# Seven products of constants on TensorE between one expert pair's down product and the next pair's gate/up

## The reference, cut to what matters

```
def per_seq(args):
    xi, gi = args
    hid = jax.nn.silu(jnp.einsum('sd,edf->sef', xi, w_gate)) * jnp.einsum('sd,edf->sef', xi, w_up)
    return jnp.einsum('sef,se,efd->sd', hid, gi, w_down)
```

## Time and profile before

| | |
|---|---|
| median of 3 runs | 774.24 us (773.31 to 775.62) |
| profiled execution, its own time | 774.24 us |
| its span, first to last instruction | 772.6 us |
| TensorE busy | 709.6 us, 92% |
| mean granted clock | 0.964 |
| moved by DMA | 150.31 MB |

### The profile page before, as it was taken

The page is one execution under the profiler, slowest core; times in us unless marked ns, Lnnn a source line. Parts: engine busy times, 40 slices in busy tenths (PEclk is TensorE's granted clock), DMA queues, the critical chain, the costliest instruction groups (busy, mean ns, idle before and its releaser), DMA issues.

```text
span 772.6 us, 10496 instructions
## 1 busy us (share of the span) xinstructions
PE 709.6 (92%) x3892; PEld 476.4 (62%) x3892; DVE 380.6 (49%) x758; ACT 279.3 (36%) x648; POOL 145.4 (19%) x126
## 2 busy tenths in 40 slices
PE   6999999999999999999999999988999786868784
PEld 5867888788888888666566688876433232323221
DVE  6876777785868723766776553471212110111100
ACT  4934633544454445544554432221212110211100
POOL 3513331330301102000120032011122111111111
PEclk9999999999999999999999999977999898989988
DMA  8333212330303122500110059798999999999972
GB/s 279 84 110 109 92 36 93 108 95 14 108 3 109 53 88 78 212 8 1 52 59 2 1 197 419 316 375 316 407 402 404 393 407 416 404 413 408 387 281 42
DMA packets 44038, 150.31 MB, mean 195 GB/s; under 512 B 11557, under 2 KB 11649, under 8 KB 32209
## 3 DMA queue, kind: packets, MB, share of 16 engines
q1 hardware_dynamic: 38384, 134.61, 45.5%
q0 software_dynamic: 4720, 8.70, 4.6%
q10 hardware_dynamic: 880, 6.30, 2.0%
HBM read 145.09 MB, written 12.88 MB: 204 GB/s over the span
## 4 chain that ended last, share of the span: by engine, by line
PE 67%; SPq 15%; DVE 6%; DMA 6%; ACT 3%; issue 2%; POOL 0%; POOLq 0%; ACTq 0%; DVEq 0%
PE bank L1093 13%; PE bank L1095 12%; PE bank L1094 12%; SPq L367 10%; PE bank L1483 6%; SPq L383 4%; DMA s_gu<-in_w_expert_up_dram 4%; PE bank L1507 3%; PE bank L1330 3%; PE bank L1302 2%; PE bank L1316 2%; PE bank L1472 2%; DVE s_wl L261 2%; PE bank L1210 2%; PE bank L1306 1%
## 5 line engine op out<-in xcount | busy, mean ns | idle before, releaser
L1483 PE MATMUL bank<-s_gu,s_xgT 128*64 128x512 f32 x448 | 110.3, 649 | 29.7 <-DMA s_gu<-in_w_expert_up_dram 29.7
L261 DVE TENSOR_TENSOR s_wl<-s_raw,s_wh 128x512 fp32r<-128x512 f32 x84 | 88.5, 1092 | 25.9 <-ACT s_wh L772 25.6
L1483 PEld LDWEIGHTS bank<-s_gu,s_xgT 128*64 128x64 f32 x448 | 36.6, 149 | 102.2 <-issue 102.2
L772 ACT ACTIVATE s_wh<-s_raw 128x512 fp32r<-128x512 f32 x120 | 74.0, 630 | 41.6 <-PE bank L1095 18.4
L1093 PE MATMUL bank<-s_wh,s_hTh 128*128 128x512 f32 x192 | 78.7, 410 | 0.0
L261 POOL TENSOR_TENSOR s_wl<-s_raw,s_wh 128x512 fp32r<-128x512 f32 x36 | 53.5, 1498 | 131.7 <-ACT s_wh L772 131.1
L1095 PE MATMUL bank<-s_wh,s_hTl 128*128 128x512 f32 x192 | 75.0, 391 | 0.0
L1094 PE MATMUL bank<-s_wl,s_hTh 128*128 128x512 f32 x192 | 74.8, 390 | 0.0
L2008 DVE COPY s_hidT<-bank 128x256 f32<-128x256 f32 x16 | 6.8, 424 | 115.1 <-PE bank L1492 115.1
L1507 PE MATMUL bank<-s_dn,s_hidT 128*64 128x512 f32 x256 | 58.5, 598 | 1.0 <-DVE s_hidT L2008 1.0
L1024 ACT ACTIVATE s_sg<-bank,s_slot_scale 128x256 f32<-128x256 f32 x16 | 7.6, 473 | 138.0 <-PE bank L1483 129.1
(11 more groups left out here) (280 smaller groups left out, 1338.4 us busy)
## 6 DMA issues: line engine op xcount, KB each, us to landing
s_dn<-in_w_expert_down_dram SPq DMA_DIRECT2D x30, 1024.0 KB, 23.8
s_gu<-in_w_expert_gate_dram SPq DMA_DIRECT2D x28, 1024.0 KB, 23.1
s_gu<-in_w_expert_up_dram SPq DMA_DIRECT2D x28, 1024.0 KB, 25.7
s_raw<-in_w_in_dram SPq DMA_DIRECT2D x88, 256.0 KB, 3.5
s_raw<-in_w_out_dram SPq DMA_DIRECT2D x32, 256.0 KB, 3.2
s_xin<-in_x_dram SPq DMA_DIRECT2D x4, 512.0 KB, 6.2
s_zs<-in_x_dram SPq DMA_DIRECT2D x1, 2048.0 KB, 10.4
s_gu<-in_w_expert_gate_dram ACTq DMA_DIRECT2D x2, 1024.0 KB, 11.1
```

The costliest lines, as they stand in the source:

```text
L261: eng.tensor_tensor(low, full, high.bitcast(F32), ALU.subtract).then_inc(sem(f"{what}_low_{low_engine(what, i)}"), 1)
L772: act.activation(wh[:, i % HL, :], raw[:, i % RAW, :], ACT.Copy).then_inc(sem("w_high"), 1)
L1483: last = pe.matmul(ps[j][r, :].rearrange("p (w f) -> p w f", w=2), m["xgT"][:, j, k, r], gu[:, half, :, k, :], start=(k == 0), stop=(k == ...
```

## The change

A helper `keep_busy(n)` issues n products with the identity and the router's weights as operands: 128 rows, 128 columns, 288 moving columns, float32, each complete by itself (start and stop), into bank 5. They wait for nothing and signal nothing. It is called once, with n = 7, behind `down` of pair 13 and so ahead of `gate_up` of pair 14.

```diff
@@ -1484,6 +1484,11 @@
+            def keep_busy(n):
+
+                for i in range(n):
+                    pe.matmul(ps[5][:, 0:KC * (NG + NE)], ident[:], wr[:].rearrange("p k e -> p (k e)"), start=True, stop=True)
+
@@ -1523,6 +1528,8 @@
                 down(p, p)
+                if p == NPAIR - 3:
+                    keep_busy(7)
                 if AHEAD <= p < NPAIR - 1:
                     gate_up(p + 1, p + 1)
```

## The result

| | before | changed |
|---|---|---|
| median of 20 runs | 774.68 us (772.15 to 777.82) | 776.10 us (773.91 to 779.87) |
| ratio | | 1.0026, 95% interval 1.0014 to 1.0038 |
| profiled execution, time and span | 774.24, 772.6 us | 775.68, 774.0 us |
| mean granted clock | 0.964 | 0.965 |

The change makes the kernel slower: by the ratio 0.26% or some 2 us, by the two medians 1.4 us. The difference is small, but it stands on the other side of no change than my forecast, and 776.1 us is outside its range.

The account below looks back on a forecast made before the run. The weights' stream was taken to bound the expert phase, with gate/up 14 also slowed by half clock. Products 0, clock -3.02, wait for the last weights +1.45 gave -1.57 us: 774.24 to 772.7 us, range 771.2 to 774.6 us.

Parts of the forecast that it names:

- What bounds the kernel: Expert phase: the weights' stream sets the pace; the end hangs on gate/up 14's weights, whose half clock lost 3.02 us.
- The seven products cost 0.48 us each and hide in the wait: Ahead of gate/up 14: 3.39 us of products within 4.2 us of TensorE's idle time, costing 0.
- The clock stays up: At gate/up 14: the clock stays at 1.00 behind the products, so it ends 3.02 us earlier.
- rival B: Ahead of gate/up 14: the clock falls anyway, gate/up 14 runs as now, 774.2 us, no change; chance 0.13.
- The cap at gate/up 15's last quarter: Middle of gate/up 15: TensorE waits 1.45 us for the last weights, leaving 1.57 us of the gain.
- No other wait takes over.: Behind gate/up 15: down 15's second load lands 0.8 us ahead of need; the last scatter comes 1.57 us earlier.
- rival A: At gate/up 15: last quarter lands before 751 us or is no limit; all 3.02 us gained, 771.2 us; chance 0.14.
- C: Ahead of gate/up 14: products outlast the wait and delay it; 775.1 us if the clock falls midway; chance 0.07.

Follow-up runs that it names:

- The four covered stalls: Changed kernel with pair 14's scatter held until gate/up 15 is done, plus products ahead of gate/ups 7, 9, 11, 12: 774.75 us, ratio 1.0001 to before.
- set 2's and set 3's held scatter: Changed kernel with pair 14's scatter held until gate/up 15 is done, measured twice against the kernel before: 773.12 us (0.9991) and 774.03 us (0.9996).
- the change (set 1): The changed kernel measured again, unaltered, on the same chip as the kernel before: 776.07 us, ratio 1.0018.

## Why the prediction was wrong

*What bounds the kernel.* Right: the landing of gate/up 14's weights starts the path, and the first fall of the clock cost what I read. The four covered stalls show the other half of it: taking away the falls further up gained nothing that could be measured.

*The seven products cost 0.48 us each and hide in the wait.* Right within 0.3 us for the seven: 14 records from 729.67 to about 733.3 us, 3.66 us for 3.39, ahead of weights that landed 0.5 us later. In two later profiles (set 2's and set 3's held scatter) the weights were there sooner, and gate/up 14 followed the products with no idle time at all.

*The clock stays up.* Right, in all nine profiles with the seven products (gate/up 14 in 7.09 us each time), though one operand is the identity; rival B is out. My comparison with the other waits was weaker than I took it: 2.35 us let the clock fall and 2.85 us did not, so 2.52 us was no bound.

The Trainium skill (TensorE: Matmul & The Clock Gate, Part 4: PE-mode transpose) says that the full clock doesn't engage for transposes, which have the identity as an operand too. These plain products did not behave so: the granted clock was 1.00 through them and gate/up 14.

*The cap at gate/up 15's last quarter.* Right in kind: a hole of 0.96 us for 1.45 forecast. From gate/up 14's start to the second half it was 17.2 us, and I had 752.52 - 735.00 = 17.5.

*Behind it: "No other wait takes over."* This step failed. I saw that the scatter would go out about 3 us earlier and that down 15's second load had 0.8 us to spare, and gave the one no effect on the other. Under rival A I even wrote that the earlier scatter shares the DMA engines with the loads, but put no price on it. The load moved by 1.6 us (22.5 to 24.1), twice what it had (and 0.3 us of that were gone, since the hole in gate/up 15 was shorter than forecast), so down 15 waited 1.1 us longer. That alone would have left 0.75 us of gain. What turned the sign is the second consequence: the added wait sits behind the silu's 1.09 us with only 0.5 us of work between, and there, or half a microsecond into down 15, the clock fell in all three profiles of the change, for 1.4 to 2.9 us. It fell in none of the ten other profiles' down 15: not where the wait was the usual 0.52 us, and not where products filled the longer one. My sum had one clock term, for the place of the change, and none for the places that it moves.

*The rivals.* The slower one that I named (C, the products in the way) was not what happened. The right one starts from rows that I had shown: scatter 14 early, down 15's load late by more than the 0.8 us, and the clock at half in down 15. (In C's working, 735.8 us is 0.8 and not 0.9 us behind the start at 735.00 us; nothing hangs on it.)

*The size.* The forecast's 772.7 us with the two missing terms, 1.1 us of wait and 1.4 to 2.9 us of half clock, gives 775.2 to 776.7 us, and 776.1 was measured. The agreement is partly luck. The hole in gate/up 15 was 0.5 us shorter than forecast, the last scatter took 0.4 us longer to land, and the median of the kernel before over 20 runs is 0.4 us above the 774.24 us from which I counted. The tails of the change are 40.15, 38.4 and 38.4 us against 37.6 us, 0.8 to 2.55 us more, and what the change saves varies as well: the fall ahead of gate/up 14 cost 3.02, 3.01 and 1.55 us in the three profiles that have it.

*How the scatter delays the load.* The ordering shows that it does: 24.1, 23.9 and 24.3 us with the scatter 14.5 us after gate/up 14's start, 23.4 at 16.0, 22.5 at 17.5, 22.1 to 22.5 in the seven profiles with it held. The DMA views of two windows show where. They give each queue's packets, MB and the time of its packets as a share of 16 engines; q1 carries the loads, q0 the scatter. The windows lie 18.5 to 20.5 and 20.5 to 22.5 us after gate/up 14's start, first in the change (set 1), then with the scatter held (set 2):

```profile
q0 software_dynamic: 58, 0.04, 12.5%
q1 hardware_dynamic: 12, 0.08, 9.8%
...
q0 software_dynamic: 7, 0.03, 7.2%
q1 hardware_dynamic: 7, 0.05, 6.2%
```

```profile
q1 hardware_dynamic: 14, 0.11, 12.6%
...
q1 hardware_dynamic: 4, 0.02, 2.0%
```

With the scatter held, the loads' tail takes 12.6% of the engines' time, which is what two of 16 would give (an estimate from this share), and is nearly over in the second window. In the change it moves 0.08 instead of 0.11 MB in the first window and still has to move 0.05 in the second, where both queues together take 13.4%. So the scatter's packets and the loads' tail are in the way of each other at these moments. That they share the same two engines fits these shares but is not shown, for the trace does not name the DMA engine of a packet.

What stays open besides: no run changed the scatter's size, and whether a kernel with the scatter held is faster than before by more than 0.1% would take more runs.

## What to carry to other kernels

A stretch of work made earlier brings its DMAs forward too: list them, and price what they meet, above all where a load has under a microsecond to spare. Where waits near the end of a program lie close together, ask for each of them whether the clock holds through it once something moves. Here the fall cost 1.4 to 2.9 us, and the added wait that let it happen 1.1 us. And where an engine waits for DMA anyway, giving it back the full clock can gain nothing: raising the mean from 0.968 to 0.980 shortened no time here.

## What was not expected of the hardware

The clock fell without one long idle time. Ahead of down 15 TensorE stood 1.09 and 1.57 us with 0.50 us of work between, and it was enough in three profiles of three. At the same place 1.09 and 0.52 us were not, in the kernel before, and neither was a single 1.98 or 2.22 us before a gate/up, nor 2.85 us in another profile. And one scatter of at most 128 rows, issued 3 us earlier, moved the landing of a 1 MB load, itself issued 15 us before the scatter, by 1.6 us.
